# ScalarE rounds the gated products in the dense-fed gates of a mixed attention, recurrence and convolution stack

## The reference

```python
qkv = jax.nn.silu(_causal_dwconv(a_qkv, a_conv_w)).astype(jnp.float32)
...
ao = _rms_norm(ao, a_norm_g).reshape(B, S, BRANCH_WIDTH).astype(dt)
y_a = ao * jax.nn.silu(a_z)
...
y_b = bu * jax.nn.silu(b_z)
...
y_c = co * jax.nn.silu(c_z)
...
ys = jnp.stack([y_a, y_b.astype(dt), y_c.astype(dt), y_d.astype(dt), y_e.astype(dt)], axis=2)
branch_out = jnp.einsum('bsnw,nwd->bsnd', ys, w_br)
```

## Time and profile before

| | |
|---|---|
| median of 3 executions | 4007.83 us (4007.68 to 4010.31) |
| the profiled execution: its own time, its span | 4009.19 us, 4007.4 us |
| mean granted TensorE clock | 0.946 |
| TensorE matmul busy | 3528.8 us (88%) |
| VectorE busy | 1816.5 us (45%) |
| ScalarE busy | 919.5 us (23%) |
| GpSimd busy | 1577.4 us (39%) |

### The profile page before, as it was taken

The page is one execution under the profiler, slowest core; times in us unless marked ns, Lnnn a source line. Parts: engine busy times, 40 slices in busy tenths (PEclk is TensorE's granted clock), DMA queues, the critical chain, the costliest instruction groups (busy, mean ns, idle before and its releaser), DMA issues.

```text
span 4007.4 us, 44134 instructions
## 1 busy us (share of the span) xinstructions
PE 3528.8 (88%) x16700; PEld 2816.8 (70%) x16700; DVE 1816.5 (45%) x2349; ACT 919.5 (23%) x1687; POOL 1577.4 (39%) x2013
## 2 busy tenths in 40 slices
PE   5898999998998899979799699669677988989988
PEld 3677898886875667757577377557566766778867
DVE  3666232226795454653521646474625344122343
ACT  2324111213012342323101322223221122120021
POOL 1453453223594224533354154243323433324423
PEclk9999989999999999989899899889888999999999
DMA  3121222112121102121121110000001111111211
GB/s 133 43 66 51 64 64 64 53 56 74 46 81 49 56 24 69 37 79 40 54 76 58 55 43 27 22 27 27 22 21 64 55 29 40 47 54 37 76 40 63
DMA packets 301494, 209.03 MB, mean 52 GB/s; under 512 B 25813, under 2 KB 277593, under 8 KB 301177
## 3 DMA queue, kind: packets, MB, share of 16 engines
q1 hardware_dynamic: 270192, 131.62, 11.8%
q10 hardware_dynamic: 31113, 74.78, 5.0%
HBM read 172.54 MB, written 33.83 MB: 51 GB/s over the span
## 4 chain that ended last, share of the span: by engine, by line
PE 69%; DVE 16%; ACT 5%; POOL 2%; issue 2%; ACTq 2%; DMA 1%; PEld 1%; DVEq 1%; PEldq 0%; POOLq 0%
PE ps L346 51%; PE ps L1247 4%; PE ps L782 3%; DVE wrk L648 3%; DVE wrk L627 2%; POOL w_lo L2332 2%; ACT wrk L810 2%; PE ps L795 1%; PE ps L521 1%; PE ps L1599 1%; POOL w_hi L2327 1%; PE ps L1873 1%; ACTq L873 1%; DVE h_lo L559 1%; DMA wrk<-away 1%
## 5 line engine op out<-in xcount | busy, mean ns | idle before, releaser
L2327 POOL TENSOR_TENSOR w_hi<-w_raw,pool_one 128x256 fp32r<-128x256 f32 x1004 | 693.9, 720 | 2377.2 <-PE ps L346 2369.5
L346 PE MATMUL ps<-h_hi,w_hi 128*128 128x512 f32 x2928 | 1210.0, 413 | 92.5 <-POOL w_lo L2332 22.4
L346 PE MATMUL ps<-h_hi,w_lo 128*128 128x512 f32 x2928 | 1156.3, 395 | 0.0
L346 PE MATMUL ps<-h_lo,w_hi 128*128 128x512 f32 x2928 | 1156.2, 395 | 0.0
L2332 POOL TENSOR_TENSOR w_lo<-w_raw,w_hi 128x256 fp32r<-128x256 f32 x1004 | 884.2, 909 | 23.1
L346 PEld LDWEIGHTS ps<-h_hi,w_hi 128*128 128x128 f32 x2928 | 559.5, 191 | 280.8 <-issue 99.5
L346 PEld LDWEIGHTS ps<-h_hi,w_lo 128*128 128x128 f32 x2928 | 558.2, 191 | 121.5
L346 PEld LDWEIGHTS ps<-h_lo,w_hi 128*128 128x128 f32 x2928 | 560.9, 192 | 111.7 <-issue 8.9
L346 PE MATMUL ps<-y_hi,w_hi 128*128 128x512 f32 (+1 forms) x896 | 345.3, 385 | 26.9 <-issue 26.2
L346 PE MATMUL ps<-y_hi,w_lo 128*128 128x512 f32 (+1 forms) x896 | 331.2, 370 | 0.0
L346 PE MATMUL ps<-y_lo,w_hi 128*128 128x512 f32 (+1 forms) x896 | 330.9, 369 | 0.0
(11 more groups left out here) (322 smaller groups left out, 3785.3 us busy)
## 6 DMA issues: line engine op xcount, KB each, us to landing
w_raw<-in_w_in SPq DMA_DIRECT2D x87, 512.0 KB
w_raw<-in_even_w_in SPq DMA_DIRECT2D x48, 512.0 KB
away<-wrk ACTq DMA_DIRECT2D x80, 256.0 KB, 2.0
wrk<-away ACTq DMA_DIRECT2D x32, 512.0 KB
w_raw<-in_odd_w_in SPq DMA_DIRECT2D x32, 512.0 KB
x_fm<-acc ACTq DMA_DIRECT2D x2, 4096.0 KB, 12.3
w_raw<-in_w_br SPq DMA_DIRECT2D x32, 256.0 KB
w_raw<-in_even_w_out SPq DMA_DIRECT2D x24, 256.0 KB
```

What stands on the lines that cost most here:

```text
L346: mm = nc.tensor.matmul(ps[:, b, 0:n], l, r, start=(k == 0 and q == 0), stop=(k == nk - 1 and q == 2))
L2327: ins = nc.gpsimd.tensor_tensor(hi, raw, one[:, 0:2], ALU.mult)
```

## The change

`gate_z` gets two more signals: `y_product`, when a product is written, and `y_rounded`, when its rounded part is. ScalarE writes the rounded part with a Copy into `y_hi` (new L423), due right after the Silu of the same half, and waits for `y_product` before it. VectorE makes the product, waits for `y_rounded` and makes the remainder; its cast and both chain links are gone. The Silu of a tile from the second on waits for `y_product` in place of `y_done`.

```diff
     def gate_z(name, r, o, bias, sz, yfirst=0, o_ready=None):
         done = sig.take("y_done", 2 * r.n)
+        product = sig.take("y_product", 2 * r.n)
+        rounded = sig.take("y_rounded", 2 * r.n)
+
+        def part(t, i):
+            return t[:, yfirst + i // 2, (i % 2) * HALF:(i % 2 + 1) * HALF]
...
                     yield when(r, j, b)
+                    i = 2 * j + b
                     out_ready(act, r.t0 + j, b)
                     if j >= 1:
-                        act.wait_ge(done.sem, done.nth(2 * (j - 1) + b))
+                        act.wait_ge(product.sem, product.nth(i - 2))
                     nc.scalar.activation(wt(sz, b), ps[:, b, :], ACT.Silu,
                                          bias=bias(j) if bias else 0.0).then_inc(dense_free[b], 1)
+                    yield when(r, j, b) + 1e-5
+                    act.wait_ge(product.sem, product.nth(i))
+                    nc.scalar.activation(part(y_hi, i), o(j, b), ACT.Copy).then_inc(rounded.sem, 1)
...
-                    ch.link(nc.vector.tensor_tensor(o(j, b), o(j, b), wt(sz, b), ALU.mult))
-                    hi = y_hi[:, yfirst + j, b * HALF:(b + 1) * HALF]
-                    lo = y_lo[:, yfirst + j, b * HALF:(b + 1) * HALF]
-                    ch.link(nc.vector.tensor_copy(hi, o(j, b)))
-                    nc.vector.tensor_tensor(lo, o(j, b), hi.bitcast(F32), ALU.subtract).then_inc(done.sem, 1)
+                    i = 2 * j + b
+                    nc.vector.tensor_tensor(o(j, b), o(j, b), wt(sz, b), ALU.mult).then_inc(product.sem, 1)
+                    dve.wait_ge(rounded.sem, rounded.nth(i))
+                    nc.vector.tensor_tensor(part(y_lo, i), o(j, b), part(y_hi, i).bitcast(F32),
+                                            ALU.subtract).then_inc(done.sem, 1)
```

## The result

| | before | after |
|---|---|---|
| median | 4007.83 us (4002.05 to 4011.12, 7 runs) | 4019.03 us (4012.38 to 4022.92, 7 runs) |
| profiled execution | 4009.2 us, span 4007.4 | 4019.0 us, span 4017.2 |
| mean granted TensorE clock | 0.946 | 0.945 |

The ratio is 1.0026, with a 95% interval from 1.0015 to 1.0038: slower by 11.2 us from median to median, and by 9.8 us from profiled execution to profiled execution.

What follows compares the result with a forecast made beforehand. It took the chain of waits, TensorE 69% and VectorE 16%, as the bound, with VectorE pacing the A gate. Seven gates 0 plus A gate +9.0 us: 4009.2 to 4018.2 profiled, 4017 us against the 4007.8 median; range 4008 to 4025 us.

Steps and rivals of the forecast that it cites:

- The loop: A gate: Copy waits for the product ahead of Square, table load and Sqrt; turn 7.9 us against 6.7, +9.0 us; chance 0.68.
- The walk: A gate, half by half from trace times: fourth Copy at 952.4, norm ends at 975.3 in place of 966.3, +9.0 us.
- No slack behind: Behind the A gate, merge and B's convolution have no gap, so everything there comes 9.0 us later.
- a term I held fixed: After the A gate's norm, ScalarE's eight loads for branch B stay the same, 4.48 us.
- Seven gates at nothing: Other gates, 56 halves: product to remainder takes 0.69 us against 0.46 to 0.88 before; cover 1.6 us, effect 0.
- The fifth Silu: A gate, fifth half: ends at 959.1 at the latest, ahead of the product starting at 959.55, just in time.
- the clock rival: A gate: gaps leave TensorE at the 1.2 GHz level, +7 us more over four turns, about 4024 us; chance 0.12.
- the signs named against the forecast: A gate reciprocals 6 to 7 us apart, low clock between 940 and 975, or TensorE awaiting a remainder elsewhere.
- Faster by VectorE's lighter load: A gate: six casts, 6 × 0.6 = 3.6 us, leave VectorE, the bound there; about 4005 us; chance 0.05.

Runs made afterwards that it cites:

- the last experiments: Changed kernel, A gate's Copy behind next Sqrt, remainder behind next norm product: 4003.36 us; same with seven other gates old: 4004.05 us; kernel before 4008.55 us.
- the bare wait: Kernel before plus, in the A gate, a ScalarE wait for the product without a Copy: 4015.86 against 4004.07 us; again 4011.04 against 4003.63 us.
- the second Copy: Kernel before with only the A gate in the new form, ScalarE writing each rounded half twice there: 4017.45 against 4003.63 us, ratio 1.0028.
- the sliver: Kernel before with only the A gate new, ScalarE rounding 8 of 512 columns and VectorE 504: 4015.34 against 4005.58 us, ratio 1.0024.

## Why the prediction held

The forecast was 4017 us, the median is 4019.03 us. Point by point:

- *The loop.* Predicted turn 7.9 us, measured 7.86; norm's end predicted at 975.3, measured 975.08; second reciprocal 926.1 (925.86), third and fourth Copy 943.5 and 952.4 (943.00, 951.75), last reciprocal 971.05 (970.94). Copy, Square, table load and Sqrt are on the chain as said. The experiments show the cause as named: with the place of the Copy alone undone, the loop is VectorE's again. The walk agrees a little better than it deserves: the fourth Copy came 0.65 us before its forecast, and a late Silu then took 0.47 us back.
- *No slack behind.* TensorE resumes at 981.24 (predicted 982.1), the 108.02 us of convolution start at 1120.71 (predicted 1122). Of the 0.9 us at TensorE, 0.65 are a term I held fixed: the eight loads took 3.83 us, 4.48 before. From the first reciprocal on, the 9.19 us of the stretch have become 8.04 us at the convolution. The span grew by 9.8 us; behind the convolution the profiles of the same kernel differ (+10.2 and +4.7 us from the first reciprocal to the end in its two takes), so the last two us are not the change's for certain. That 4019.03 lies 2 us from 4017 is partly luck: the forecast took single executions to vary by 1.5 us, with three of them at hand, while 35 of them vary by 16 us, and the same kernel measured again was 7.3 us above the one before, not 11.2.
- *Seven gates at nothing.* Their product-to-remainder time is 0.69 + 0.70 = 1.39 us from start to start, as worked out; no row of TensorE waits for a remainder of `gate_z`. The 56 halves came to 1.0006 (0.9997 to 1.0015) and to 0.9997 (0.9987 to 1.0007).
- *The fifth Silu*, which I had as just in time (959.1, the product at 959.55), was late: it started at 958.73 and ran to 959.42, and the product, at 959.45, had waited 0.47 us for it. What held it up is a piece of the clock rival: after its longest gap, 3.49 us, TensorE made the norm's sums at a granted clock of 0.50, in 2.07 us where 1.13 had been enough.
- *The clock rival* did not come as a whole, but it was not empty either: a clock well below 1.00 between 940 and 975 was among the signs named against the forecast, and it was there for some 2 us. The clock is 0.97 over 922 to 975.1, 1.00 in the stretches behind gaps of 1.90 and 2.63 us, and 1.00 again from 956.5 on. In the kernel with only the A gate changed the low clock lasted longer: 0.50 from 957.9 to 964.5, so that the fifth Silu waited 4.09 us for its matmuls and the product 1.94 us for the Silu. That is the 1.4 us by which its stretch exceeds the full change's. The forecast priced the lower clock at 7 us for four turns; what the runs show is one turn, at 0.47 to 1.94 us.
- *Faster by VectorE's lighter load* was wrong as it stood, as argued: VectorE stood where the cast had been. But the mechanism exists. It needs the two moves of the last experiments, which give VectorE something to do in that time, and then pays 4.5 to 5 us by the medians, 2.8 to 3.5 us in the stretch.
- Wait and work were never split in the prediction. My later expectations for the stretch, 4 to 9 us for the bare wait and 3.5 to 5 us for the second Copy, were both too high, for the reasons shown with them. The text ahead of the sliver calls the last two steps of the bare wait the same as before; they were not quite, as said above.

What stays open: the bare wait has +3.6 us in its stretch, +3.5 and +3.2 us to the end in the profiles, and yet +11.8 and +7.4 us in the medians. The clock covers part of it: as an estimate, executions of one kernel are some 3 us longer per 0.001 of mean clock (16.4 us from 0.947 to 0.942 in the 35 of before), and the first take of the bare wait had 0.9441 against 0.9452 beside it. The second had 0.9447 against 0.9445, and there 5.8 us are left between the means. No profile shows the rest.

## What to carry to other kernels

Moving work to an idle engine is priced by its place in that engine's queue more than by its length: here, in a quiet half, the Copy cost 0.47 us and the wait ahead of it 1.55 us, because it stopped an engine that had been running ahead for the very loop that feeds it. Put an instruction that waits for the end of a round behind the ones that start the next round, and give the engine that waits for it the next round's work first; the same change then gained some 5 us in place of losing 7 to 11. And where executions differ by as much as the effect, compare a stretch with fixed ends inside the profiles: it repeated within 0.1 us where a kernel ran twice (and within 1.4 us where only the gate was the same), while medians of whole kernels moved by 4.

## What was not expected of the hardware

- A wait on ScalarE need not hold the table load behind it in the program. With the bare wait the load ran at 954.61 and the Sqrt waited until 956.35; where a Square or a Copy carried the wait, the table load stood behind. Nor is the reverse a rule: with the Copy behind the next root, one table load (at 926.17) itself waited 1.89 us for a norm product. Which instruction carries a wait has to be looked up in the queue.
- Narrowing the Copy from 512 columns to 8 brought it from 0.63 to 0.21 us, and its start-to-start step from 0.54 to 0.11 us.
- TensorE's granted clock: gaps of 1.90 and 2.63 us between halves left it at 1.00, after the third one, 3.49 us, it was 0.50 (the lower level, 1.2 GHz) for the norm's two sums. The length of the gap alone does not decide it: in both takes of the bare wait the clock was 0.50 behind a gap of 2.16 us (2.17 in the second), the sums taking 2.06 and 2.08 us, with 1.00 up to the gap. The busy time by stretch of the changed kernel:

```profile
936.00:944.00 8.00, 5.23 (x20) 3.68 (x20) 5.53 (x5) 5.14 (x7) 0.00 (x0) 1.00 0.17 51
944.00:952.00 8.00, 5.25 (x20) 3.69 (x20) 5.94 (x4) 4.26 (x6) 5.02 (x7) 1.00 0.00 0
952.90:955.10 2.20, 2.07 (x2) 0.50 (x2) 0.89 (x2) 2.16 (x3) 0.08 (x1) 0.50 0.35 89
955.10:959.00 3.90, 3.87 (x15) 3.20 (x16) 3.84 (x2) 1.28 (x2) 0.00 (x0) 0.84 0.08 21
```

- One kernel's executions differ together with the clock they are granted: twelve of the changed kernel on one chip went from 4008.81 us at a mean clock of 0.947 to 4024.37 us at 0.942, and the 35 of the kernel before beside them from 3999.47 us at 0.947 to 4015.85 us at 0.942.
